# A two-layer decoder trunk on one core: VectorE alone sums all 2048 columns of the first weighted-sum stage

## The chip, the core and the metric

The program runs on one core of a Trainium2 chip. The metric is the device time of one execution in microseconds (us), lower is better; the median of several runs is taken. Engines: TensorE (PE), VectorE (DVE), ScalarE (ACT), GpSimd (POOL) and SyncE (SP). TensorE's granted clock is printed as a share of 2.4 GHz.

## The reference, cut to what matters

The trunk has 256 tokens of width 2048 (two blocks of 128 tokens) and two layers: a mixer, then a PEER expert layer, each added to the residual. All data is float32. The change touches the expert layer, in which each token picks 128 experts (8 heads by 16) and sums their value rows:

```python
def one_block(xb):                                   # xb: 128 tokens x 2048
    q = (xb @ w_q).reshape(BLOCK, PEER_HEADS, 2, PEER_HALF)
    s = jnp.einsum('thcd,hcnd->thcn', q, sub_keys)
    top_s, top_i = lax.top_k(s, PEER_TOPK)           # 16 of 128, twice per head
    ...                                              # 16 of the 256 pairs: eidx, gate g
    ue = u[eidx]                                     # 128 experts per token, rows of 2048
    ve = v[eidx]
    act = gelu(einsum('thkd,td->thk', ue, xb))
    return einsum('thk,thkd->td', g * act, ve)
```

## The kernel before, in words

Tokens lie on the 128 partitions. For one block of tokens and one layer, expert slot n (0 to 127) is one gather: GpSimd issues an indirect DMA (line 511) that brings, for each of the 128 tokens, one row of 2048 floats, 1 MB in all, into one of the 8 buffers of `ring`. A gather waits until its buffer has been used: `ring_free` (counted by VectorE) and, where TensorE reads the ring too, `pe_freed`.

The gathers form one sequence of eight phases of 128 slots, two for each of (layer 0, block 0), (layer 0, block 1), (layer 1, block 0), (layer 1, block 1). Even phases gather rows of `u`: VectorE takes a dot product with `H` for each slot (`expert_dots`, line 1391). Odd phases gather rows of `v`: the rows are summed, weighted, into the residual `X` (`expert_sum`, `weigh`, line 1400). The first weighted-sum stage is phase 1, the second and third are phases 3 and 5, and the last is phase 7.

In phases 1, 3 and 5 the sum is shared. `SHARED` gives the first shared slot. Ahead of it VectorE adds all 2048 columns of a row. From it on VectorE adds columns 0 to 1023, and TensorE adds columns 1024 to 2047 into two banks of PSUM (`weigh_part`, line 995: two matmuls for each slot, with a diagonal matrix of the slot's weights as the stationary operand). ScalarE makes these diagonals (`diagonals`, line 629), one for each slot, in 8 buffers. After slot 127 VectorE waits for TensorE and adds the two banks to `X` (line 1471), which counts `merged`; the next layer's work on ScalarE (`squares`) and TensorE (`spread_gain`) waits for `merged`.

Between the slots VectorE also does what the other block of tokens needs. `paced` hands out one piece of such work after every fourth slot at the places listed; in phase 1 these are 13 pieces of the routing of block 1 (`route`, `experts`, `gates`), after slots 35, 39, 47, 51, 59, 63, 71, 75, 83, 87, 95, 99 and 107. The last of them counts `routed`. SP, which streams the weight matrices through four buffers (`load_rows` and the loads of `w_in1` at line 430), waits for `routed` at the start of layer 1; GpSimd waits for it ahead of the gathers of phase 2; so does TensorE. On ScalarE the exponential of the gates (`gate_exp`) stands in program order behind the diagonals of slots 32 to 99, and the diagonals of slots 100 to 127 behind it.

Of the kernel before, what the change touches and what calls it, by code (L numbers as in the profile page):

```python
# [35 lines left out]
SLOTS = PEER_H * PEER_K  # L36
# [27 lines left out]

SHARED = {1: 32, 3: 24, 5: 24}
DVE_COLS = 1024
XBANKS = (1, 2, 3)
DIAGS = 8  # L70
# [43 lines left out]
def shared_before(phase, n=0):  # L114

    return sum(SLOTS - j for p, j in SHARED.items() if p < phase) + (max(n - SHARED[phase], 0) if phase in SHARED else 0)

# [6 lines left out]
def program(nc, x, positions, norm_mix0, w_in0, sinks0, conv_w0, w_out0, norm_ffn0, peer_wq0,  # L124
# [10 lines left out]
    with ctx:  # L135
# [3 lines left out]
        def sem(name):  # L139
            return ctx.enter_context(nc.semaphore(name))  # L140
# [105 lines left out]
        def bank(i, n=1, w=512):  # L246
            return ps[:, i * 512:(i + n - 1) * 512 + w]
# [9 lines left out]
        def landings(phase, n):  # L257

            return 16 * ((phase * SLOTS + n) // RING + 1)
# [37 lines left out]
        wgt_ready, diag_ready, pe_freed, merged = sem("wgt_ready"), sem("diag_ready"), sem("pe_freed"), sem("merged")  # L297
# [227 lines left out]
        def _(act):  # L525
# [30 lines left out]
            def copy_all_queries(layer, b):  # L556

                act.wait_ge(chunk_done, chunk_before(f"wq{layer}", b) + 1)
                for c in range(4):
                    nc.scalar.copy(Q1[:, c * CH:(c + 1) * CH], bank(c)).then_inc(chunk_copied, 1)  # L560
                copy_transposes(f"q{layer}", b)
# [51 lines left out]
            def gate_exp(layer, b):  # L613
                act.wait_ge(best_ready, layer * NB + b + 1)
                nc.scalar.activation(gate[:, b, :], gate[:, b, :], ACT.Exp).then_inc(gexp_done, 1)
# [6 lines left out]
            def diagonals(phase, n0, n1):  # L622

                act.wait_ge(wgt_ready, (phase + 1) // 2)
                for n in range(n0, n1):
                    k = shared_before(phase, n)
                    if k >= DIAGS:
                        act.wait_ge(pe_freed, k - DIAGS + 1)
                    nc.scalar.activation(diag[k % DIAGS], ident[:, :], ACT.Identity,  # L629
                                         scale=wgt[:, n:n + 1]).then_inc(diag_ready, 1)  # L630
# [64 lines left out]
            copy_transposes("h1", 1)  # L695
            gelus(0, 0)
            copy_all_queries(0, 1)
            diagonals(1, SHARED[1], 100)
            gate_exp(0, 1)
            diagonals(1, 100, SLOTS)  # L700

            for b in range(NB):
                act.wait_ge(merged, b + 1)
# [28 lines left out]
                copy_all_queries(1, b)  # L732
                diagonals(3 + 2 * b, SHARED[3 + 2 * b], 100)
                gate_exp(1, b)
# [21 lines left out]
        def _(pe):  # L756
# [228 lines left out]

            def weigh_part(phase):

                n0 = SHARED[phase]
                for n in range(n0, SLOTS):
                    k = shared_before(phase, n)  # L990
                    pe.wait_ge(diag_ready, k + 1)
                    pe.wait_ge(landed[n % RING], landings(phase, n))
                    for c in range(2):
                        at = DVE_COLS + c * CH
                        last = nc.tensor.matmul(bank(4 + c), diag[k % DIAGS], ring[:, n % RING, at:at + CH],  # L995
                                                start=(n == n0), stop=(n == SLOTS - 1))
                    last.then_inc(pe_freed, 1)

            def key_scores(keys, count, phase):
                for g in range(2 * PEER_H):  # L1000
                    last = nc.tensor.matmul(ps[:, g * NKEY:(g + 1) * NKEY], PQT[:, g, :], keys[:, g, :],
                                            start=True, stop=True)
                last.then_inc(rs_done, 1)
                weigh_part(phase)
                pe.wait_ge(routed, count)
# [158 lines left out]
        def _(dve):  # L1164
# [24 lines left out]
            def norm(n):  # L1189
                blocks = NORMS[n][1]  # L1190
                inverse_root(slice(blocks[0], blocks[-1] + 1), D, sq_done, norm_before(n + 1), var_ready,
                             root_ready, n + 1)
                if n in (0, 1, 3):
                    dve.wait_ge(gain_loaded, 16 * min(n + 1, 2))
                else:
                    dve.wait_ge(gain_spread, max(n - 2, 1))
                if n == 8:
                    dve.wait_ge(lifted, 12)
                spread = last_gain if n == 8 else gain[:, :] if n in (0, 1, 3) else bank(4 * ((n + 1) % 2), 4)
                for b in blocks:  # L1200
                    V.scalar_tensor_tensor(out=H[:, b, :], in0=X[:, b, :],  # L1201
                                           scalar=stat[:, 5, b:b + 1],
                                           in1=spread, op0=ALU.mult, op1=ALU.mult).then_inc(h_ready, 1)
                dve.wait_ge(h_ready, norm_before(n + 1))

            def rope(v, cos, sin, tmp):

                _, blocks, heads, dim = v.shape
                half = dim // 8
                a, b_ = v[:, :, :, 0:half], v[:, :, :, half:2 * half]  # L1210
                step = HALF_ROT // half
                shape = [P, blocks, heads, half]
                cs = cos[:, :, 0:HALF_ROT:step].unsqueeze(2).broadcast_to(shape)
                sn = sin[:, :, 0:HALF_ROT:step].unsqueeze(2).broadcast_to(shape)
                t = [tmp[:, i, 0:blocks * heads * half].rearrange("p (b h d) -> p b h d", b=blocks, h=heads)
                     for i in range(4)]
                V.tensor_tensor(t[0], a, cs, ALU.mult)
                V.tensor_tensor(t[1], b_, sn, ALU.mult)
                V.tensor_tensor(t[2], b_, cs, ALU.mult)
                link(V.tensor_tensor(t[3], a, sn, ALU.mult))  # L1220
                V.tensor_tensor(a, t[0], t[1], ALU.subtract)
                link(V.tensor_tensor(b_, t[2], t[3], ALU.add))
# [172 lines left out]
            def weigh(b, phase, i, s, weight):  # L1395
                dve.wait_ge(ring_free, i * PEER_K + (phase * SLOTS + s + RING))
                dve.wait_ge(landed[s % RING], i * 32 + 16 * (phase * SLOTS // RING + s // RING + 1))
                cols = DVE_COLS if i * PEER_K + s >= SHARED.get(phase, SLOTS) else D
                acc = last_x if phase == 7 else X[:, b, 0:cols]
                V.scalar_tensor_tensor(out=acc, in0=ring[:, s % RING, 0:cols], scalar=weight, in1=acc,  # L1400
                                       op0=ALU.mult, op1=ALU.add).then_inc(ring_free, 1)

            def last_weigh(phase):

                n = SLOTS - 1
                dve.wait_ge(ring_free, phase * SLOTS + n + RING)
                dve.wait_ge(landed[n % RING], landings(phase, n))
                for i in range(2):
                    cols = slice(i * 1024, (i + 1) * 1024)
                    last = V.scalar_tensor_tensor(out=last_x[:, cols], in0=ring[:, n % RING, cols], scalar=wgt[:, n:n + 1],  # L1410
                                                  in1=last_x[:, cols], op0=ALU.mult, op1=ALU.add)
                    last.then_inc(half_summed, 1)
                dve.wait_ge(half_summed, 2)
                dve.nop(nofuse=True).then_inc(ring_free, 1)
# [37 lines left out]
            def expert_sum(b, phase, between=None):  # L1452

                if between:
                    for n in range(SLOTS):
                        weigh(b, phase, n // PEER_K, n % PEER_K, wgt[:, n:n + 1])
                        if n % 4 == 3:
                            between(n // 4)
                else:
                    with dve.Fori(0, PEER_H - 1) as i:  # L1460
                        for s in range(PEER_K):
                            weigh(b, phase, i, s, wgt[:, bass.ds(i * PEER_K + s, 1)])
                    norm(8)
                    for n in range(SLOTS - PEER_K, SLOTS - 1):
                        weigh(b, phase, n // PEER_K, n % PEER_K, wgt[:, n:n + 1])
                    last_weigh(phase)
                dve.wait_ge(ring_free, (phase + 1) * SLOTS + RING)
                if phase in SHARED:
                    dve.wait_ge(pe_freed, shared_before(phase, SLOTS))
                    cols = X[:, b, DVE_COLS:D]  # L1470
                    V.tensor_tensor(cols, part, cols, ALU.add).then_inc(merged, 1)
                    dve.wait_ge(merged, (phase + 1) // 2)
# [208 lines left out]
```

## Time and profile before

| | |
|---|---|
| median of 3 runs | 3301.86 us (3299.7 to 3306.68) |
| the profiled execution's own time | 3302.28 us |
| its span | 3300.3 us |
| VectorE busy | 2401.2 us, 73% |
| TensorE busy | 1683.4 us, 51% |
| GpSimd busy | 1514.8 us, 46% |
| ScalarE busy | 333.7 us, 10% |
| moved by DMA | 1319.82 MB, mean 400 GB/s |

The span runs from the first to the last instruction; the execution's own time is 2 us longer. The busy shares are averages over stages that differ. Each phase is read by itself: the DMA share and the GB/s of a stretch say whether the transfers were at their rate, and the idle time in front of an engine's instructions, with what ended it, says for whom it waited.

### The profile page before, as it was taken

To read this page: it belongs to the slowest core of one execution; us is meant where nothing else is said; L and a number is where in the kernel's file an instruction comes from. 1 tells how busy PE (TensorE), PEld (TensorE's weight loads), DVE (VectorE), ACT (ScalarE), POOL (GpSimd) and SP (SyncE) were. 2 spreads that over 40 slices of the span, in tenths; PEclk is the share of its full clock that TensorE was granted. 3 is DMA by queue.
4 is the path that set the end of the run, shared out by engine and by line. 5 is a ranking of instruction groups with operands and counts; after the bars stand their busy time and mean duration, and the time that the engine had idled before them with its cause. 6 is when DMAs were issued, how large, how long until landed. Compare 5 with 4: busy or idle time off the path is not lost.

```text
span 3300.3 us, 18324 instructions
## 1 busy us (share of the span) xinstructions
PE 1683.4 (51%) x5280; PEld 844.2 (26%) x5280; DVE 2401.2 (73%) x2771; ACT 333.7 (10%) x783; POOL 1514.8 (46%) x1042
## 2 busy tenths in 40 slices
PE   7995466575577662547377763556277700000000
PEld 4955322232222231323122232332122200000000
DVE  1129674676777568866977577966976689999999
ACT  1110000110111101100111112110011100000000
POOL 0105342353565545644766544644756643333332
PEclk9997799788899996779699977788699955555555
DMA  9669799899999999999999999999999999999997
GB/s 336 229 242 411 295 421 420 349 394 421 422 421 421 419 420 411 411 416 421 422 421 420 421 419 414 388 422 422 421 422 421 422 422 422 421 422 421 422 422 332
DMA packets 215948, 1319.82 MB, mean 400 GB/s; under 512 B 23536, under 2 KB 23600, under 8 KB 70832
## 3 DMA queue, kind: packets, MB, share of 16 engines
q0 software_dynamic: 147728, 1074.86, 78.7%
q1 hardware_dynamic: 68128, 243.86, 18.7%
q8 instruction: 43, 0.70, 0.1%
q14 instruction: 49, 0.40, 0.0%
HBM read 1316.54 MB, written 2.10 MB: 400 GB/s over the span
## 4 chain that ended last, share of the span: by engine, by line
issue 29%; POOL 21%; DMA 20%; PE 16%; DVE 12%; ACT 2%; DVEq 0%; POOLq 0%; PEldq 0%; SPq 0%; ACTq 0%
POOL ring L511 21%; DMA ring<-in_peer_v,eidx 10%; DVE ps L1400 9%; PE ps L995 7%; DMA A<-in_w_in 4%; PE ps L795 3%; PE ps L811 3%; DMA ring<-in_peer_u,eidx 3%; DMA A<-in_peer_wq 2%; PE ps L945 1%; PE ps L791 1%; ACT A L629 1%; DVE X L1400 1%; ACT KT L629 1%; PE ps L1016 0%
## 5 line engine op out<-in xcount | busy, mean ns | idle before, releaser
L511 POOL DMA_INDIRECT ring<-in_peer_u,eidx x512 | 762.8, 1490 | 965.2 <-DVE dots L1391 797.0
L1391 DVE CUSTOM_DVE_ANT_0 kdup<-ring,H 128x2048 bf16<-128x2048 f32 x384 | 880.0, 2292 | 286.8 <-DMA ring<-in_peer_u,eidx 279.4
L511 POOL DMA_INDIRECT ring<-in_peer_v,eidx x512 | 734.2, 1434 | 641.0 <-DVE ps L1400 189.9
L1400 DVE SCALAR_TENSOR_TENSOR X<-ring,wgt,X 128x1024 f32<-128x1024 f32 (+1 forms) x384 | 578.6, 1507 | 263.6 <-DMA ring<-in_peer_v,eidx 253.7
L995 PE MATMUL ps<-ring,KT 128*128 128x512 f32 x608 | 302.0, 622 | 209.9 <-DMA ring<-in_peer_v,eidx 147.3
L995 PE MATMUL ps<-ring,A 128*128 128x512 f32 x608 | 297.1, 611 | 92.2 <-ACT A L629 48.7
L1400 DVE SCALAR_TENSOR_TENSOR ps<-ring,wgt,ps 128x2048 f32<-128x2048 f32 x127 | 299.1, 2355 | 18.4 <-DVE ps L1400 5.2
L1391 DVE CUSTOM_DVE_ANT_0 kdup<-ring,ps 128x2048 bf16<-128x2048 f32 x128 | 292.8, 2288 | 21.2 <-DMA ring<-in_peer_u,eidx 15.6
L995 PEld LDWEIGHTS ps<-ring,KT 128*128 128x128 f32 x608 | 106.4, 194 | 403.6 <-issue 244.7
L774 PE MATMUL ps<-ident,gainT 128*128 128x128 f32 x192 | 25.5, 298 | 322.5 <-DVE wgt L1447 319.2
L995 PEld LDWEIGHTS ps<-ring,A 128*128 128x128 f32 x608 | 103.1, 189 | 286.2 <-ACT A L629 125.1
L774 PEld LDWEIGHTS ps<-ident,gainT 128*128 128x128 f32 x192 | 24.6, 211 | 326.4 <-issue 326.4
L629 ACT ACTIVATE KT<-ident,wgt 128x128 f32<-128x128 f32 x152 | 60.1, 403 | 433.6 <-PE ps L995 433.6
L945 PE MATMUL ps<-PR,HT 128*128 128x512 f32 x144 | 69.3, 621 | 65.9 <-issue 37.5
L851 PE MATMUL ps<-PR,HT 128*128 128x512 f32 x192 | 87.7, 602 | 21.1 <-DMA PR<-in_peer_wq 19.8
L811 PE MATMUL ps<-HT,ring 128*128 128x128 f32 x768 | 88.7, 278 | 1.6 <-ACT PR L642 1.0
L629 ACT ACTIVATE A<-ident,wgt 128x128 f32<-128x128 f32 x152 | 59.7, 401 | 291.7 <-PE ps L995 291.7
L811 PEld LDWEIGHTS ps<-HT,ring 128*128 128x128 f32 x768 | 87.4, 194 | 3.4 <-ACT PR L642 1.9
L901 PE MATMUL ps<-ident,A 128*128 128x128 f32 x96 | 19.4, 359 | 121.0 <-ACT A L595 120.1
L759 PE MATMUL ps<-ident,H 128*128 128x128 f32 x140 | 28.4, 387 | 97.1 <-DVE H L1201 96.0
L488 POOL TENSOR_TENSOR PR<-PR 128x1024 f32<-128x1024 f32 x1 | 2.3, 2347 | 129.6 <-ACT PR L651 129.6
L1520 DVE TENSOR_TENSOR X<-ps,X 128x512 f32<-128x512 f32 x4 | 2.8, 691 | 76.8 <-PEq L781 76.8
(291 smaller groups left out, 1990.7 us busy)
## 6 DMA issues: line engine op xcount, KB each, us to landing
ring<-in_w_in SPq DMA_DIRECT2D x18, 2048.0 KB, 12.3
PR<-in_peer_wq SPq DMA_DIRECT2D x32, 1024.0 KB, 16.1
PR<-in_w_out SPq DMA_DIRECT2D x24, 1024.0 KB, 13.7
PR<-in_w_in SPq DMA_DIRECT2D x24, 768.0 KB, 14.6
ring<-in_w_out SPq DMA_DIRECT2D x8, 2048.0 KB, 9.4
A<-in_peer_wq SPq DMA_DIRECT2D x16, 1024.0 KB, 16.1
A<-in_w_out SPq DMA_DIRECT2D x12, 1024.0 KB, 12.4
A<-in_w_in SPq DMA_DIRECT2D x12, 768.0 KB, 14.6
```

The source lines that it names most:

```text
L511: pool.indirect_dma_start(ring[:, n % RING, :], None, table, bass.IndirectOffsetOnAxis(eidx[:, b, n:n + 1], 0)).then_inc(landed[n % RING], 16)
L629: nc.scalar.activation(diag[k % DIAGS], ident[:, :], ACT.Identity, scale=wgt[:, n:n + 1]).then_inc(diag_ready, 1)
L759: last = nc.tensor.transpose(ps[:, bank0 * 512 + i * P:bank0 * 512 + (i + 1) * P], s, ident[:, :])
L774: last = nc.tensor.matmul(ps[:, at:at + P], gainT[:, i, k:k + 1].broadcast_to([P, P]), ident[:, :], start=True, stop=True)
L791: last = nc.tensor.matmul(bank(4 * (m % 2) + g, w=tokens), tile[:, k, g * P:(g + 1) * P], lhs[:, kk, :], **flags)
L795: last = nc.tensor.matmul(bank(4 * (m % 2) + b, w=width), lhs[:, kk, b * P:(b + 1) * P], tile[:, k, 0:width], **flags)
L811: last = nc.tensor.matmul(ps[:, at:at + P], wtile(slot)[:, k, c:c + P], HT1[:, 8 * t + k, :], start=(t == k == 0), stop=(t == 1 and k == 7))
L851: last = nc.tensor.matmul(bank(bank0 + c), lhs[:, k, :], rows[n % WSLOTS][:, c * CH:(c + 1) * CH], start=(k == 0), stop=(k == KT_ - 1))
L945: last = nc.tensor.matmul(bank(bank0 + c), HT1[:, k, :], rows_l0[n % WSLOTS][:, c * CH:(c + 1) * CH], start=(k == 0), stop=(k == KT_ - 1))
L995: last = nc.tensor.matmul(bank(4 + c), diag[k % DIAGS], ring[:, n % RING, at:at + CH], start=(n == n0), stop=(n == SLOTS - 1))
L1391: V.tensor_tensor_reduce(out=junk, in0=ring[:, s % RING, :], in1=last_h if phase == 6 else H[:, b, :], scale=1.0, scalar=0.0, op0=ALU.mult ...
L1400: V.scalar_tensor_tensor(out=acc, in0=ring[:, s % RING, 0:cols], scalar=weight, in1=acc, op0=ALU.mult, op1=ALU.add).then_inc(ring_free, 1)
```

## The change

`SHARED` loses its entry for phase 1, so in that phase every slot counts as unshared: VectorE adds all 2048 columns of all 128 rows. TensorE's loop over the slots of phase 1 is empty, ScalarE's two calls of `diagonals` for phase 1 are gone, and instead of the addition that merged TensorE's half, an empty VectorE instruction counts `merged` after the last slot. Phases 3 and 5 stay as they are (their diagonals are counted from 0 in place of 96, a multiple of 8, so the same buffers serve the same slots).

```diff
-SHARED = {1: 32, 3: 24, 5: 24}
+SHARED = {3: 24, 5: 24}
@@ ScalarE
             copy_all_queries(0, 1)
-            diagonals(1, SHARED[1], 100)
             gate_exp(0, 1)
-            diagonals(1, 100, SLOTS)
@@ TensorE, weigh_part
-                n0 = SHARED[phase]
+                n0 = SHARED.get(phase, SLOTS)
                 for n in range(n0, SLOTS):
@@ VectorE, expert_sum
                 dve.wait_ge(ring_free, (phase + 1) * SLOTS + RING)
+                if phase == 1:
+                    dve.nop(nofuse=True).then_inc(merged, 1)
                 if phase in SHARED:
                     dve.wait_ge(pe_freed, shared_before(phase, SLOTS))
```

Line numbers of the changed kernel are lower by 2 or 3 behind the ScalarE edit. On VectorE, at the start of phase 1, the rows of the kernel before are these (`X<-ring,wgt,X` is the weighted addition of a slot, the others are pieces of the routing):

```order
L1400 SCALAR_TENSOR_TENSOR X<-ring,wgt,X 128x2048 x32
L1400 SCALAR_TENSOR_TENSOR X<-ring,wgt,X 128x1024 x4
L1278 MAX A<-ps 128x8 x16
L1400 SCALAR_TENSOR_TENSOR X<-ring,wgt,X 128x1024 x4
L1282 MAX_INDEX A<-A,ps 128x8 x16
```

and of the changed kernel these:

```order
L1398 SCALAR_TENSOR_TENSOR X<-ring,wgt,X 128x2048 x36
L1276 MAX A<-ps 128x8 x16
L1398 SCALAR_TENSOR_TENSOR X<-ring,wgt,X 128x2048 x4
L1280 MAX_INDEX A<-A,ps 128x8 x16
L1398 SCALAR_TENSOR_TENSOR X<-ring,wgt,X 128x2048 x8
```

The pieces stand behind the same slots; the additions from slot 32 on have 2048 columns in place of 1024. On the same engine at the end of phase 1, before:

```order
L1350 TENSOR_TENSOR gate<-gate,gsum 128x128
L1400 SCALAR_TENSOR_TENSOR X<-ring,wgt,X 128x1024 x20
L1471 TENSOR_TENSOR X<-ps,X 128x1024
L1391 ISA kdup,dots<-ring,H 128x2048
L1391 ISA dots 128x1
```

and in the changed kernel:

```order
L1348 TENSOR_TENSOR gate<-gate,gsum 128x128
L1398 SCALAR_TENSOR_TENSOR X<-ring,wgt,X 128x2048 x20
L1389 ISA kdup,dots<-ring,H 128x2048
L1389 ISA dots 128x1
```

The merging addition is gone (the empty instruction in its place stands in no row), and the first dot product of phase 2 (`kdup,dots<-ring,H`) follows the last slot. On TensorE the changed kernel goes from the routing's scores (L999) straight to the work that waits for `merged` (L772):

```order
L862 MATMUL ps<-ident,HT 128x128 x16
L999 MATMUL ps<-PR 128x128 x16
L772 MATMUL ps<-ident,gainT 128x128 x16
L757 MATMUL ps<-ident,H 128x128 x16
L1092 MATMUL ps<-PR,HT 128x512
```

Before, 192 matmuls of 512 columns (L995), two for each of 96 slots, stood between the second and the third of these rows; the trace counts each float32 matmul twice, so that it shows 384 of them. Nothing else moved on TensorE.

## Rows read from the trace of the kernel before

**Rows 1.** Windows: stretch, length; PE, PEld, DVE, ACT, POOL; clock, DMA, GB/s.

```profile
891.60:1141.10 249.50, 188.71 (x384) 65.87 (x384) 174.26 (x302) 36.48 (x90) 143.33 (x97) 0.99 1.01 421
1142.00:1180.00 38.00, 24.48 (x88) 15.31 (x88) 36.27 (x37) 5.83 (x8) 27.87 (x15) 0.82 1.01 420
1142.00:1530.00 388.00, 199.61 (x636) 110.08 (x637) 295.67 (x324) 48.21 (x118) 197.77 (x118) 0.77 1.01 415
2650.00:2968.00 318.00, 0.43 (x2) 0.46 (x3) 295.61 (x266) 3.47 (x6) 119.88 (x129) 0.50 1.01 422
1300.00:1340.00 40.00, 5.55 (x30) 5.36 (x30) 39.13 (x51) 1.50 (x8) 28.31 (x15) 0.59 0.97 380
```

**Rows 2.** Page, section 2: 40 slices of the span, busy tenths and GB/s.

```profile
DMA  9669799899999999999999999999999999999997
GB/s 336 229 242 411 295 421 420 349 394 421 422 421 421 419 420 411 411 416 421 422 421 420 421 419 414 388 422 422 421 422 421 422 422 422 421 422 421 422 422 332
```

**Rows 3.** Waits of VectorE, 785 to 1142 us: total, times, longest.

```profile
DVE X L1400 <- DMA ring<-in_peer_v,eidx: 95.5, 69, 2.6
...
DVE X L1471 <- PE ps L995: 0.8, 1, 0.8
```

**Rows 4.** Waits of VectorE, 1142 to 1530 us.

```profile
DVE kdup L1391 <- DMA ring<-in_peer_u,eidx: 81.8, 45, 2.7
...
DVE stat L1181 <- ACT A L711: 1.8, 1, 1.8
```

**Rows 5.** Timeline of VectorE, phase 1: start, duration, instruction, idle before.

```profile
791.62 23.84 DVE L1400 SCALAR_TENSOR_TENSOR X<-ring,wgt,X 128x2048 f32<-128x2048 f32 x10
...
894.09 1.28 DVE L1400 SCALAR_TENSOR_TENSOR X<-ring,wgt,X 128x1024 f32<-128x1024 f32 x1 [1.20 <-DMA ring<-in_peer_v,eidx]
...
900.25 3.26 DVE L1278 MAX8 A<-ps 128x8 f32<-128x128 f32 x16
```

**Rows 6.** Timeline of VectorE, end of phase 1.

```profile
1092.62 1.29 DVE L1400 SCALAR_TENSOR_TENSOR X<-ring,wgt,X 128x1024 f32<-128x1024 f32 x1 [2.39 <-DMA ring<-in_peer_v,eidx]
1096.18 1.29 DVE L1400 SCALAR_TENSOR_TENSOR X<-ring,wgt,X 128x1024 f32<-128x1024 f32 x1 [2.27 <-DMA ring<-in_peer_v,eidx]
...
1136.53 1.28 DVE L1400 SCALAR_TENSOR_TENSOR X<-ring,wgt,X 128x1024 f32<-128x1024 f32 x1 [1.21 <-DMA ring<-in_peer_v,eidx]
1139.01 1.28 DVE L1400 SCALAR_TENSOR_TENSOR X<-ring,wgt,X 128x1024 f32<-128x1024 f32 x1 [1.20 <-DMA ring<-in_peer_v,eidx]
1141.12 1.23 DVE L1471 TENSOR_TENSOR X<-ps,X 128x1024 f32<-128x1024 f32 x1 [0.82 <-PE ps L995]
1142.38 2.29 DVE L1391 CUSTOM_DVE_ANT_0 kdup<-ring,H 128x2048 bf16<-128x2048 f32 x1
```

**Rows 7.** Timeline of TensorE, phase 1.

```profile
891.65 6.91 PE L995 MATMUL ps<-ring,KT 128*128 128x512 f32 x12 [22.26 <-DMA ring<-in_peer_v,eidx]
...
937.35 1.95 PE L995 MATMUL ps<-ring,KT 128*128 128x512 f32 x4 [0.53 <-ACT KT L629]
```

**Rows 8.** Line 1400 alone, same columns as rows 1 for VectorE.

```profile
891.60:1141.10 249.50, 123.34 (x96) 0.99 1.01 421
```

**Rows 9.** Groups of VectorE, 785 to 1142 us: count | busy, mean | idle.

```profile
L1400 DVE SCALAR_TENSOR_TENSOR X<-ring,wgt,X 128x1024 f32<-128x1024 f32 x96 | 123.3, 1285 | 74.3 <-DMA ring<-in_peer_v,eidx 72.9
L1400 DVE SCALAR_TENSOR_TENSOR X<-ring,wgt,X 128x2048 f32<-128x2048 f32 x32 | 75.3, 2352 | 24.6 <-DMA ring<-in_peer_v,eidx 22.5
```

**Rows 10.** Issues of SP, 1060 to 1142 us, then the DMA view.

```profile
1082.92 0.89 SPq L430 DMA_DIRECT2D PR<-in_w_in  x2
...
PR<-in_w_in SPq DMA_DIRECT2D x2, 848.0 KB, 14.5
A<-in_w_in SPq DMA_DIRECT2D x1, 848.0 KB, 25.0
MT<-in_w_in SPq DMA_DIRECT2D x1, 848.0 KB, 31.2
```

**Rows 11.** Timeline of GpSimd, phase 1: gather issues.

```profile
794.24 2.93 POOL L511 DMA_INDIRECT ring<-in_peer_v,eidx  x1 [11.39 <-DVE X L1400]
797.48 2.08 POOL L511 DMA_INDIRECT ring<-in_peer_v,eidx  x1 [0.30 <-issue]
799.87 2.08 POOL L511 DMA_INDIRECT ring<-in_peer_v,eidx  x1 [0.30 <-issue]
...
1076.36 1.01 POOL L511 DMA_INDIRECT ring<-in_peer_v,eidx  x1 [0.30 <-issue]
1077.68 1.01 POOL L511 DMA_INDIRECT ring<-in_peer_v,eidx  x1 [0.30 <-issue]
...
1091.72 0.94 POOL L511 DMA_INDIRECT ring<-in_peer_v,eidx  x1 [2.20 <-PE ps L995]
```

**Rows 12.** Timeline of GpSimd, phase 7.

```profile
3258.38 0.94 POOL L511 DMA_INDIRECT ring<-in_peer_v,eidx  x1 [1.46 <-DVE ps L1400]
```

**Rows 13.** Line 511, issue to landing: 1300 to 1340 us, then the whole span.

```profile
DMA to landing us min/median/max: 9.2/9.9/14.3
...
DMA to landing us min/median/max: 6.5/17.0/38.0
```

**Rows 14.** TensorE, `spread_gain` after phase 1 and after long idling.

```profile
1142.49 3.81 PE L774 MATMUL ps<-ident,gainT 128*128 128x128 f32 x32 [1.48 <-DVE X L1471]
...
2967.57 6.56 PE L774 MATMUL ps<-ident,gainT 128*128 128x128 f32 x32 [319.19 <-DVE wgt L1447]
```

## The prediction

> **What bounds the kernel now.** I read the windows first. From 891.6 to 1141.1 us, which are slots 32 to 127 of phase 1, the DMA share is 1.01 at 421 GB/s, while VectorE is busy 174.26 of 249.5 us. It is much the same in the phases behind (415 GB/s from 1142 to 1530 us, 422 from 2650 to 2968 us) [rows 1], and in most of the 40 slices [rows 2]. So the kernel is bound by its transfers: from phase 1 on the DMA engines have next to no idle time in which they could catch up, and a microsecond in which they starve is a microsecond of the end. The waits say the same from the other side: in phase 1 VectorE idles 95.5 us for gathers to land, and 0.8 us for TensorE at the merge [rows 3]. VectorE starts a slot every 2.49 us (1136.53, 1139.01) and works 1.28 us of it [rows 6]; TensorE takes 1.95 us for its half [rows 7]. Both are faster than the gather.
>
> The question is therefore one only: can VectorE by itself keep up with a gather every 2.49 us, with its pieces of routing among the slots?
>
> **The change part by part.**
>
> *VectorE's additions.* A full-width slot, back to back, costs 23.84 / 10 = 2.384 us [rows 5], against 2.352 us for the instruction alone [rows 9]. That is 0.1 us under the gather's 2.49. So slots without a piece among them only just keep up. The 96 slots from 32 on take 96 x 2.384 = 228.9 us, where they take 123.34 us now [rows 8].
>
> *The pieces.* In the same window VectorE is busy 174.26 us in all [rows 1], 123.34 of them line 1400 [rows 8]; the other 174.26 - 123.34 = 50.9 us are the routing. They now lie in the 1.2 us holes ahead of each slot [rows 5, 6] and cost nothing. With full-width additions the holes are gone, and they stand on the path.
>
> *Sum on VectorE.* 228.9 + 50.9 = 279.8 us from 891.65 us, where TensorE takes up slot 32 [rows 7], so the last slot is done at 1171.4 us. Today the last slot is done at 1139.01 + 1.28 = 1140.3, and the first dot product of phase 2 starts at 1142.38, behind TensorE's last half (0.82 us of idle) and the merge (1.23 us) [rows 6]. These 2.1 us go away, and nothing is late in their place: the row that is needed next has landed by then, or is the gather priced below. So phase 2 starts 1171.4 - 1142.4 = 29 us later by VectorE's own time.
>
> *What the ring can take up.* Eight buffers let the transfers run ahead of VectorE, but no more than that. They run ahead from slot 35 on, and after some ten slots with pieces all buffers hold landed rows and the DMA engines go idle. This buys nothing at the end of the phase, since there the transfers are the slower side again: after slot 107 come 20 slots without a piece (47.7 us on VectorE), and beside their gathers SP brings the four tiles of `w_in1`, 4 x 848 KB [rows 10], which at 421 GB/s are 8.3 us. 20 x 2.49 + 8.3 = 58 us of transfers in 48 us of VectorE: the ring is drained by slot 127, as today.
>
> *How late a freed buffer is filled.* After starving, the transfers need one gather's latency to start again. Where VectorE is the slow side today, a gather lands 9.9 us after its issue at the median, against 17.0 us when the queue is full and 6.5 us at the least [rows 13]. I ran the recursion for both (a gather lands at the later of freed + latency and last landing + 2.49; VectorE starts at the later of landed and free). Its first form, which counts each piece's overlap with its neighbour twice (13 x 0.11 = 1.4 us), gives a DMA idle time of 31.4 us with a latency of 6.6 and 34.8 with 10; less 1.4 us it is 30.0 and 33.4 us. Its bound from below is VectorE's 29 us. I take 31 us, nearer to VectorE's own sum, which comes from rows without a model.
>
> *GpSimd.* Its issue of a gather takes 2.08 us while VectorE runs full-width additions from `ring` and `X`, 1.0 us between short instructions [rows 11], and 0.94 us where VectorE's accumulator is in PSUM [rows 12]. So one gather is issued for each full-width addition (2.08 + 0.30 = 2.38 us), as many as buffers come free: it adds latency, which the last step holds, and no rate. The Trainium skill ("SBUF — State Buffer", Who interferes with whom) says that a VectorE instruction with two SBUF inputs contends only with GpSimd instructions that read SBUF, and infers that descriptor generation, which writes, is not held. The rows above disagree: the issue is held. By the page the latency would be the short one, 6.5 us, and the sum 30; by the row it is 31 to 33.
>
> *ScalarE and TensorE.* The 96 diagonals and 192 matmuls cost nothing now, hidden under the transfers (DMA share 1.01 [rows 1]), and give nothing when they go. The exponential of the gates no longer waits behind diagonals; the routing piece that needs it comes after slot 107, long after, so 0. TensorE will have idled for some 300 us when phase 2 begins. After idling as long, `spread_gain` takes 6.56 us, with the granted clock at 0.50 (1.2 GHz) up to there, in place of 3.81 [rows 1, 14]. The norm that needs them comes after four dot products (over 9 us), so this is hidden. The first matmuls of `w_in1` behind it may be late by 2 to 4 us; VectorE's wait in the low-rank norm, 1.8 us now [rows 4], can grow by that, but VectorE idles 81.8 us for gathers in that phase [rows 4] and the ring covers a stall of a few us. I take 0 and keep 4 us for the upper end.
>
> *Is it given back later?* VectorE's time is: it has the 81.8 us. The transfers' time isn't: in the phases behind they run at 415 to 422 GB/s with or without the change [rows 1].
>
> *Total.* 3302.28 + 31 = 3333.3 us for the profiled execution; the median lies 0.4 us lower, so 3333 us. Own range: 29 us less 3 of error in the sum at the bottom, 33.4 + 4 and 1 at the top: 3328 to 3340.
>
> **The rivals.**
>
> *A. The ring and the later idle time take it all up, no change.* For it: 95.5 us of idle VectorE in the phase. The idle time here is 74.3 us at the shared slots [rows 9], the work added 96 x (2.384 - 1.285) = 105.5 us, so 105.5 - 74.3 = 31 us do not fit, which is the same sum by another way. For it to be hidden the transfers would have to have slack behind, against rows 1. Then the time is 3302.3 less the 2.1 us of the merge: 3300. Chance 0.05.
>
> *B. GpSimd becomes the bound.* An issue held by VectorE needs 2.08 + 0.30 = 2.38 us, just VectorE's pitch. If it kept missing its turn and every issue took 2.93 us, as the first one of such a run does [rows 11], plus 0.30, then 96 slots take 96 x 3.23 = 310 us in place of 249.5, less the merge: +58, 3360. Against it: ten slots at full width keep 2.38 without a miss [rows 5, 11], and short instructions let it catch up at 1.3 us each [rows 11]. It decides from the point where issues fall behind the freed buffers by more than the ring. Chance 0.04.
>
> *C. Faster.* TensorE holds the ring. Around 1091.72 us GpSimd waits 2.20 us for TensorE, not for VectorE [rows 11], and slots come every 3.6 us there (1092.62, 1096.18 [rows 6]), eight of them. If that were TensorE's doing, taking it out would give 8 x (3.6 - 2.49) = 8.9 us and the 2.1 of the merge, if VectorE kept up: 3291. It decides if VectorE's lag stays under the ring's eight slots. Against it: the tiles of `w_in1` are issued at 1082.92 us [rows 10] and their 8.3 us are the same 8.9 us; TensorE waits for the gather too. Chance 0.03.
>
> *D. A cold TensorE delays phase 2.* It would show in phase 2 as longer waits of VectorE for ScalarE and TensorE; from 1300 to 1340 us the transfers already drop to 380 GB/s with VectorE busy 39.13 of 40 us [rows 1], so a late mixer there would starve them. TensorE is busy 24.48 us from 1142 to 1180 us at a mean clock of 0.82 [rows 1]; at 0.50 throughout that is 24.48 x 0.82 / 0.50 = 40 us, 16 us more. If 10 of them weren't covered: 3343. Chance 0.08.
>
> **How the numbers follow.** The forecast has 0.80, A 0.05, B 0.04, C 0.03, D 0.08. The range reaches from 3323 to 3344: the forecast's own range, D, and 5 us below for a routing that overlaps more than its busy time shows. A measurement of this kernel tells 0.2% (6.6 us) from no change. Slower by more: forecast, B, D, 0.92 in all. Within it: A, 0.05. Faster: C, 0.03.
>
> **What would show it.** In the profile after, line 1400 has 128 instructions of 2048 columns in phase 1 with a mean of 2.35 us and, from slot 36 on to about 115, no wait for a gather; the wait for `in_peer_v` in phase 1 falls from 95.5 to some 25 us. GpSimd waits for VectorE ahead of most issues. The transfers fall below 421 GB/s between some 970 and 1130 us, with 31 us of starving in all (about 375 GB/s over the stretch from 891 to 1171 us), and are at 421 again by 1140. The first dot product of phase 2 starts near 1172 us, and each phase behind it ends 29 to 33 us later than before, with its own length kept. The prediction is wrong if VectorE still waits for gathers between the pieces; if phase 2 or a later one becomes shorter, so that some is given back; or if the stretch from slot 32 to slot 127 takes over 290 us, which would point to GpSimd.

## The result and the profile after

The changed kernel takes 3336.73 us (median of 4 runs, 3332.82 to 3344.16), the kernel before 3302.8 us beside it. The ratio is 1.0104, with a 95% interval of 1.0091 to 1.0117. That is 34 us slower, where 31 were forecast. The profiled execution took 3334.28 us, 32.0 us more than that of before, with a span of 3332.5 us.

The windows of the changed kernel (columns as in [rows 1]) cut the stretch of slots 32 to 127 into pieces of about 40 us, and the last row is phase 2 at the same length as in [rows 1]:

```profile
891.60:930.00 38.40, 0.00 (x0) 0.00 (x0) 37.61 (x61) 0.00 (x0) 26.54 (x14) 0.50 1.01 422
930.00:970.00 40.00, 0.00 (x0) 0.00 (x0) 39.50 (x63) 0.00 (x0) 27.77 (x15) 0.50 0.93 375
970.00:1010.00 40.00, 0.00 (x0) 0.00 (x0) 39.50 (x55) 0.00 (x0) 27.27 (x14) 0.50 0.83 325
1010.00:1050.00 40.00, 0.00 (x0) 0.00 (x0) 39.57 (x54) 0.00 (x0) 27.37 (x14) 0.50 0.95 371
1050.00:1090.00 40.00, 0.00 (x0) 0.00 (x0) 39.47 (x35) 0.31 (x1) 25.95 (x12) 0.50 0.90 364
1090.00:1130.00 40.00, 0.00 (x0) 0.00 (x0) 39.33 (x22) 0.00 (x0) 29.21 (x13) 0.50 0.74 299
1130.00:1173.00 43.00, 0.00 (x0) 0.00 (x0) 41.68 (x18) 0.01 (x1) 37.51 (x19) 0.50 1.02 421
...
1173.00:1561.00 388.00, 204.25 (x630) 113.32 (x630) 294.15 (x323) 48.21 (x118) 200.60 (x119) 0.75 1.01 418
```

The third busy figure is VectorE's: 37.6 us of 38.4, then 39.5 of 40, with no room left. The last figure is the transfers' rate. It holds at 422 GB/s for the first 38 us, in which the ring absorbs the lag, falls for 200 us, and is back at 421 in the last 43 us, where no pieces lie. Where the rate was 421 throughout in [rows 1], the missing part comes to 40 x (5 - (375 + 325 + 371 + 364 + 299) / 421) = 35 us.

Phase 2 starts only 30.9 us later, so some 4 us of the missing transfers are not paid for there. From the weights of phase 1 to the first dot product of phase 2 the changed kernel moves 145.58 MB and the kernel before 147.70 MB, and almost all of the 2.1 MB between them are gathers (5.0 us at 421 GB/s). Phase 2 moves 1.0 MB more than before in the same 388 us (162.20 against 161.20 MB, the 418 GB/s against 415). Almost all of that (0.9 MB) is moved in one place: from 1307 to 1346 us the kernel before transfers at 379 GB/s, with VectorE busy 38.21 of 39 us, and the changed kernel has 402 GB/s from 1338 to 1377 us, the same place 31 us later. There the transfers had time to spare, and 2 to 3 us of the lag go into it.

The waits of VectorE from 785 to 1173 us answer to [rows 3]:

```profile
DVE X L1398 <- DMA ring<-in_peer_v,eidx: 23.0, 10, 2.6
DVE wgt L1447 <- ACT score L619: 5.9, 1, 5.9
```

Of 95.5 us of waiting for gathers 23.0 are left, ten waits, and these lie ahead of slot 32. The timeline of VectorE at the end of the phase answers to [rows 6]:

```profile
1116.65 7.13 DVE L1398 SCALAR_TENSOR_TENSOR X<-ring,wgt,X 128x2048 f32<-128x2048 f32 x3
1123.69 0.28 DVE L1346 TENSOR_REDUCE gsum<-gate 128x8 f32<-128x128 f32 x1
1124.01 0.20 DVE L1347 RECIPROCAL gsum<-gsum 128x8 f32<-128x8 f32 x1
1124.25 0.29 DVE L1348 TENSOR_TENSOR gate<-gate,gsum 128x128 f32<-128x128 f32 x1
1124.57 48.32 DVE L1398 SCALAR_TENSOR_TENSOR X<-ring,wgt,X 128x2048 f32<-128x2048 f32 x20
1173.14 2.29 DVE L1389 CUSTOM_DVE_ANT_0 kdup<-ring,H 128x2048 bf16<-128x2048 f32 x1 [0.25 <-DMA ring<-in_peer_u,eidx]
```

The first dot product of phase 2 starts at 1173.14 us in place of 1142.38. Of GpSimd this is what the issues look like around a piece of routing (937.4 to 941.7 us; the first addition behind it ends at 944.1), and below it, from the view of line 511, how long a gather took to land, from 900 to 1100 us:

```profile
936.18 2.09 POOL L511 DMA_INDIRECT ring<-in_peer_v,eidx  x1 [0.30 <-issue]
938.58 0.93 POOL L511 DMA_INDIRECT ring<-in_peer_v,eidx  x1 [0.30 <-issue]
944.37 2.93 POOL L511 DMA_INDIRECT ring<-in_peer_v,eidx  x1 [4.86 <-DVE X L1398]
```

```profile
DMA to landing us min/median/max: 6.6/8.0/16.3
```

Behind the piece GpSimd waits 4.86 us for VectorE to free a buffer. A gather lands 8.0 us after its issue at the median, near the least of the kernel before (6.5 us) and far from its median of 17.0 [rows 13].

### The profile page after: what moved, and what is told of

Same layout as the page of the kernel before. It is cut to its first block, busy times and chain, and to the rows that moved or that the text cites. A ratio compares the mean times of both kernels' runs of the same rounds, so it can differ in the third digit from the quotient of the medians.

```text
span 3332.5 us, 17114 instructions
## 1 busy us (share of the span) xinstructions
PE 1505.3 (45%) x4896; PEld 784.4 (24%) x4896; DVE 2502.4 (75%) x2770; ACT 296.3 (9%) x687; POOL 1583.4 (48%) x1042
## 4 chain that ended last, share of the span: by engine, by line
DMA 25%; issue 22%; DVE 19%; POOL 17%; PE 15%; ACT 2%; DVEq 0%; POOLq 0%; PEldq 0%; SPq 0%; ACTq 0%
POOL ring L511 17%; DMA ring<-in_peer_u,eidx 10%; DVE ps L1398 9%; DMA ring<-in_peer_v,eidx 8%; DVE X L1398 5%; PE ps L993 5%; DMA HT<-in_w_in 5%; PE ps L793 3%; PE ps L809 3%; DMA HT<-in_peer_wq 2%; DVE kdup L1389 1%; PE ps L943 1%; PE ps L789 1%; PE ps L978 0%; ACT KT L629 0%
## 5 line engine op out<-in xcount | busy, mean ns | idle before, releaser
L511 POOL DMA_INDIRECT ring<-in_peer_u,eidx x512 | 773.1, 1510 | 952.2 <-DVE dots L1389 785.3
L1389 DVE CUSTOM_DVE_ANT_0 kdup<-ring,H 128x2048 bf16<-128x2048 f32 x384 | 880.0, 2292 | 287.2 <-DMA ring<-in_peer_u,eidx 279.8
L511 POOL DMA_INDIRECT ring<-in_peer_v,eidx x512 | 792.4, 1548 | 619.3 <-DVE ps L1398 191.0
L1398 DVE SCALAR_TENSOR_TENSOR X<-ring,wgt,X 128x1024 f32<-128x1024 f32 (+1 forms) x384 | 681.0, 1774 | 193.8 <-DMA ring<-in_peer_v,eidx 181.0
L772 PE MATMUL ps<-ident,gainT 128*128 128x128 f32 x192 | 26.6, 305 | 624.0 <-DVE wgt L1445 319.4
L993 PE MATMUL ps<-ring,KT 128*128 128x512 f32 x416 | 205.9, 620 | 159.0 <-DMA ring<-in_peer_v,eidx 115.5
L993 PE MATMUL ps<-ring,A 128*128 128x512 f32 x416 | 203.3, 611 | 61.2 <-ACT A L629 35.7
L772 PEld LDWEIGHTS ps<-ident,gainT 128*128 128x128 f32 x192 | 25.7, 218 | 627.4 <-issue 627.4
L993 PEld LDWEIGHTS ps<-ring,KT 128*128 128x128 f32 x416 | 72.1, 192 | 291.6 <-issue 176.0
L993 PEld LDWEIGHTS ps<-ring,A 128*128 128x128 f32 x416 | 70.4, 189 | 194.0 <-ACT A L629 93.2
L849 PE MATMUL ps<-PR,HT 128*128 128x512 f32 x192 | 93.9, 638 | 20.7 <-DMA PR<-in_peer_wq 19.4
L943 PE MATMUL ps<-PR,HT 128*128 128x512 f32 x144 | 69.8, 623 | 64.5 <-issue 37.6
L629 ACT ACTIVATE KT<-ident,wgt 128x128 f32<-128x128 f32 x104 | 41.1, 401 | 312.8 <-PE ps L993 312.8
L978 PE MATMUL ps<-PR,MT 128*128 128x512 f32 x128 | 59.2, 617 | 2.7 <-ACT MT L611 2.7
```

The lines of the kernel that those rows point to most:

```text
L511: pool.indirect_dma_start(ring[:, n % RING, :], None, table, bass.IndirectOffsetOnAxis(eidx[:, b, n:n + 1], 0)).then_inc(landed[n % RING], 16)
L772: last = nc.tensor.matmul(ps[:, at:at + P], gainT[:, i, k:k + 1].broadcast_to([P, P]), ident[:, :], start=True, stop=True)
L849: last = nc.tensor.matmul(bank(bank0 + c), lhs[:, k, :], rows[n % WSLOTS][:, c * CH:(c + 1) * CH], start=(k == 0), stop=(k == KT_ - 1))
L943: last = nc.tensor.matmul(bank(bank0 + c), HT1[:, k, :], rows_l0[n % WSLOTS][:, c * CH:(c + 1) * CH], start=(k == 0), stop=(k == KT_ - 1))
L978: last = nc.tensor.matmul(bank(4 + c), MT1[:, k, :], rows_l1[n % WSLOTS][:, c * CH:(c + 1) * CH], start=(k == 0), stop=(k == KT_ - 1))
L1389: V.tensor_tensor_reduce(out=junk, in0=ring[:, s % RING, :], in1=last_h if phase == 6 else H[:, b, :], scale=1.0, scalar=0.0, op0=ALU.mult ...
```

## The experiments

Each ratio is to the kernel before, timed on the same chip. The profiled executions differ by up to 9 us in what they take before phase 1, which no edit here touches. So the traces are compared by the length of phase 1, from the moment VectorE computes the weights of phase 1 (`wgt<-score,gate`) to the first dot product of phase 2. That is 1142.38 - 791.29 = 351.1 us before and 1173.14 - 791.15 = 382.0 us in the changed kernel, 30.9 more. Each such length comes from one execution. Those of the runs that leave phase 1 at its old speed lie between 349.9 and 351.8 us, so a difference under 2 us says nothing.

### Both engines' work, and VectorE at full width

```diff
 # the kernel before, VectorE's additions
-cols = DVE_COLS if i * PEER_K + s >= SHARED.get(phase, SLOTS) else D
+cols = DVE_COLS if phase > 1 and i * PEER_K + s >= SHARED.get(phase, SLOTS) else D
 # the merge of phase 1: an empty instruction that counts merged
```

> The kernel before, but in phase 1 VectorE adds all 2048 columns from slot 32 on, while TensorE and ScalarE still do their 96 diagonals and 192 matmuls (the sums are dropped: an empty instruction in place of the merge). Theory: what costs is VectorE's width alone. Phase 2 starts at 1173 to 1176 us in place of 1142.4, and the time is that of the changed kernel, ratio to before 1.009 to 1.012 (3333 to 3342 us). Rival (a TensorE that idled and is cold, or work whose cover is gone, makes up part of the loss): with TensorE busy as before, the ratio is under 1.006 (under 3323 us).

Measured: 3335.66 us, ratio 1.0098 (1.0079 to 1.0118), phase 1 of 1174.86 - 791.51 = 383.4 us. Its window answers to the first of [rows 1]:

```profile
891.60:1141.10 249.50, 174.84 (x340) 62.58 (x340) 245.92 (x290) 34.46 (x86) 170.53 (x84) 0.94 0.90 361
```

TensorE is at work (174.84 us) with a clock of 0.94 and ScalarE makes its diagonals, and still the transfers fall to 361 GB/s. The whole loss is there with nothing taken from the other engines. VectorE's width makes it. Phase 1 is 1.4 us longer than in the changed kernel, and the phases behind it are 3.0 us shorter (2997.61 - 1174.86 = 1822.8 us from the first dot product of phase 2 to the weights of phase 7, against 1825.8). In phase 1 the difference is two short waits for gathers behind slot 32, 1.5 us in all; why they are there, and why the phases behind are shorter, no run says. The medians (3335.66 and 3336.73 us) can't be told apart.

### TensorE's part left out, VectorE at half width

```diff
 # the changed kernel, VectorE's additions
-cols = DVE_COLS if i * PEER_K + s >= SHARED.get(phase, SLOTS) else D
+cols = DVE_COLS if i * PEER_K + s >= (32 if phase == 1 else SHARED.get(phase, SLOTS)) else D
```

> The changed kernel, but VectorE adds only columns 0 to 1023 from slot 32 of phase 1 on, as before, and nobody adds the other 1024 (this half of the first sum is left out for 96 slots). TensorE and ScalarE idle in phase 1. Theory: TensorE's and ScalarE's part was hidden under the transfers, so without it the time is that of before less at most the 2.1 us of the merge: ratio 0.998 to 1.001, DMA at 421 GB/s through the phase. Rival cold TensorE: phase 2 becomes longer, ratio 1.002 or more. Rival (TensorE held the ring around 1090 us): 3291 us, ratio 0.997 or less.

Measured: 3302.61 us, ratio 0.9994 (0.9984 to 1.0003), phase 1 of 349.9 us. In the trace of this kernel VectorE's wait in phase 1 and the windows are:

```profile
DVE X L1398 <- DMA ring<-in_peer_v,eidx: 95.4, 69, 2.6
```

```profile
891.60:1141.10 249.50, 0.00 (x0) 0.00 (x0) 175.73 (x303) 0.31 (x1) 112.81 (x98) 0.50 1.01 421
```

```profile
1142.00:1180.00 38.00, 26.73 (x88) 17.69 (x87) 35.43 (x35) 5.42 (x8) 27.81 (x14) 0.75 1.02 421
```

The same wait as before the change (95.4 against 95.5 us), the same rate of transfers: TensorE's and ScalarE's part cost nothing in phase 1. TensorE enters phase 2 from a clock of 0.50, runs at 0.75 in its first 38 us where it ran at 0.82, and is busy 26.73 us for 24.48 [rows 1]. These 2 us don't show in the time: from the first dot product of phase 2 to the weights of phase 7 pass 2968.96 - 1142.74 = 1826.2 us, against 1825.4 before, and this length lies between 1822.8 and 1826.6 us in all the traces here. This puts an end to the rival of a cold TensorE at the size that it was given (10 us), and, since taking TensorE off the ring gains nothing, to the one that it held the gathers.

### VectorE with 1536 columns, TensorE with 512

```diff
 # the kernel before; in phase 1 from slot 32 on
-cols = DVE_COLS if ... else D
+cols = (1536 if phase == 1 else DVE_COLS) if shared else D
-for c in range(2):                              # TensorE
+for c in range(1 if phase == 1 else 0, 2):
 # the merge of phase 1 adds columns 1536 to 2047 only
```

> The kernel before, but in phase 1 VectorE adds 1536 columns from slot 32 on and TensorE 512 (one matmul a slot). Theory: VectorE's sum is 96 x about 1.85 + 50.9 = 228 us, under the 249 us of the transfers, so the ring covers nearly all: phase 2 starts 0 to 3 us later, ratio 1.000 to 1.001. Rival (each added column costs, in proportion, as where GpSimd's issue is held for the length of each addition): half of the loss, 15 to 17 us, ratio 1.005.

Measured: 3301.9 us, ratio 0.9995 (0.9986 to 1.0005), phase 1 of 351.8 us. The group of the 96 additions, columns as in [rows 9], and the window:

```profile
L1401 DVE SCALAR_TENSOR_TENSOR X<-ring,wgt,X 128x1536 f32<-128x1536 f32 x96 | 174.5, 1818 | 24.1 <-DMA ring<-in_peer_v,eidx 21.6
```

```profile
891.60:1141.10 249.50, 174.96 (x190) 43.01 (x190) 225.38 (x302) 36.50 (x90) 162.57 (x97) 0.61 1.00 415
```

Half of the added work was added, 174.5 - 123.3 = 51 us, and phase 1 is 0.7 us longer, no more than the traces scatter. VectorE's sum of 174.5 + 50.9 = 225 us lies under the 249.5 of the transfers. The price is a threshold, not a proportion. The rate of 415 GB/s instead of 421 is 249.5 x 6 / 421 = 3.6 us of missing transfers, so here too some 3 us of them are not paid for. TensorE's granted clock was 0.61 here, and its matmuls took longer, 174.96 us for half as many; this cost nothing either.

### Full width from slot 108 on

```diff
 SHARED = {1: 32, 3: 24, 5: 24}
+END = {1: 108, 3: 128, 5: 128}      # used by both engines, the diagonals and the counts
```

> The kernel before, but the sharing of phase 1 ends at slot 107, the last slot with a piece of routing behind it: slots 108 to 127 are full width on VectorE. Theory: a full-width slot costs 2.384 us against 2.49 us a gather, so where no piece lies among the slots and the tiles of w_in1 slow the gathers further, full width is free: phase 2 starts 0 to 1.5 us later, ratio 0.999 to 1.001. Rival (full width costs wherever it stands): 20/96 of the loss, 6.5 us, ratio 1.002.

Measured: 3302.63 us, ratio 0.9998 (0.9988 to 1.0007), phase 1 of 350.4 us. VectorE's timeline in this kernel:

```profile
1083.08 4.81 DVE L1402 SCALAR_TENSOR_TENSOR X<-ring,wgt,X 128x2048 f32<-128x2048 f32 x2 [0.48 <-DMA ring<-in_peer_v,eidx]
1088.69 2.35 DVE L1402 SCALAR_TENSOR_TENSOR X<-ring,wgt,X 128x2048 f32<-128x2048 f32 x1 [0.81 <-DMA ring<-in_peer_v,eidx]
...
1110.34 2.35 DVE L1402 SCALAR_TENSOR_TENSOR X<-ring,wgt,X 128x2048 f32<-128x2048 f32 x1 [1.20 <-DMA ring<-in_peer_v,eidx]
1114.07 27.00 DVE L1402 SCALAR_TENSOR_TENSOR X<-ring,wgt,X 128x2048 f32<-128x2048 f32 x11 [1.38 <-DMA ring<-in_peer_v,eidx]
```

VectorE still waits for gathers between full-width additions. The long waits lie where the tiles of `w_in1` slow the gathers to one in 3.6 us; the last 11 additions start 2.46 us apart on average ((27.00 - 2.35) / 10), nearer to the gathers' 2.49 than to VectorE's 2.384. So in the last 20 slots, where no piece of routing lies, full width is free.

### Sharing from slot 64 on

```diff
-SHARED = {1: 32, 3: 24, 5: 24}
+SHARED = {1: 64, 3: 24, 5: 24}
```

> The kernel before, but phase 1 is shared from slot 64 on in place of 32: 32 more slots are full width, six pieces of routing lie behind them (after slots 35 to 63). Theory, by the recursion of the prediction (a gather lands at the later of freed buffer + 9 to 10 us and last landing + 2.49 us): VectorE needs 32 x 2.4 + 23.8 = 100.6 us where the gathers need 80.5, so 20 us too many; the ring holds back some 10 of them; phase 2 starts 9 to 10 us later and the ratio is 1.003. Rival (the whole excess counts, the ring gives nothing): 20 us, ratio 1.006. Rival (proportional to slots): 32/96 of 31 us, 10 us, which this run can't tell from the first; the run with a full-width tail does that.

Measured: 3310.72 us, ratio 1.0031 (1.0020 to 1.0042), phase 1 of 1149.01 - 789.97 = 359.0 us, 8.0 more than before; 9 to 10 were expected. The windows show where:

```profile
930.00:970.00 40.00, 0.00 (x0) 0.00 (x0) 39.50 (x63) 0.00 (x0) 28.09 (x14) 0.50 0.94 375
970.00:1010.00 40.00, 25.14 (x49) 9.23 (x50) 39.43 (x79) 4.82 (x12) 24.86 (x18) 0.89 0.92 359
1010.00:1141.00 131.00, 95.63 (x197) 33.20 (x196) 86.64 (x100) 18.82 (x46) 71.22 (x51) 1.00 1.01 421
```

By the sum above VectorE has 20 us too much, and the kernel loses 8: in this one trace the ring takes up 12 us, once. VectorE idles 44 of the 131 us behind (86.64 busy) and the loss stays. Idle time of VectorE afterwards gives nothing back, since the transfers are at their rate (421 GB/s) there.

### The sum in PSUM

```diff
 # the changed kernel; ScalarE copies X to four banks before phase 1, and back after it
-acc = last_x if phase == 7 else X[:, b, 0:cols]
+acc = last_x[:, 0:cols] if phase in (1, 7) else X[:, b, 0:cols]
```

> The changed kernel, but the sum of phase 1 is kept in four banks of PSUM (ScalarE copies X there beforehand and back afterwards), as phase 7 does, so that the additions have one input in SBUF, and GpSimd's issue should take 0.94 us instead of 2.08. Theory: VectorE's pitch is the same (2.39 us), so the loss is the same but for some of the latency: phase 2 starts at 1170 to 1174 us, ratio to before 1.008 to 1.010. Rival (GpSimd's held issues make a good part of the loss): phase 2 starts before 1165 us, ratio 1.006 or less.

Measured: 3332.88 us, ratio 1.0091 (1.0076 to 1.0107), phase 1 of 1173.67 - 792.01 = 381.7 us, 0.3 less than in the changed kernel. The timeline of GpSimd at the same place as above:

```profile
936.24 0.94 POOL L512 DMA_INDIRECT ring<-in_peer_v,eidx  x1 [1.45 <-DVE ps L1405]
938.63 0.94 POOL L512 DMA_INDIRECT ring<-in_peer_v,eidx  x1 [1.45 <-DVE ps L1405]
945.26 0.94 POOL L512 DMA_INDIRECT ring<-in_peer_v,eidx  x1 [5.69 <-DVE ps L1405]
```

GpSimd's issue is 0.94 us again in place of 2.08 and 2.93, and the ratio can't be told from that of the changed kernel (their intervals overlap). The held issue is real, and it is not what the kernel waits for. The time from issue to landing is the same as well, 7.9 us against 8.0 (median, 900 to 1100 us), so this run doesn't say what a shorter latency would be worth.

### The pieces packed

```diff
-ROUTE_AT = (8, 9, 11, 12, 14, 15, 17, 18, 20, 21, 23, 24, 26)
+ROUTE_AT = (8, 9, 10, 11, 12, 13, 14, 15, 16, 17, 18, 19, 20)
```

> The changed kernel, but the 13 pieces of routing come after every fourth slot from 35 to 83, not spread out to 107. The count of instructions is the same. Theory, by the recursion: while the pieces last the transfers starve, and behind slot 83 VectorE is the faster side again and idles, so a little is lost more: phase 2 starts at 1175 to 1178 us, ratio 1.010 to 1.011. Rival 1 (only VectorE's sum counts, wherever the pieces lie): 1173 us, 1.0095. Rival 2 (the 8.3 us of w_in1 tiles, issued earlier since the last piece is earlier, fill time in which the gathers starve): the ratio falls to 1.0075 (3327 us).

Measured: 3342.51 us, ratio 1.0115 (1.0099 to 1.0130), phase 1 of 1184.59 - 798.96 = 385.6 us, 3.6 more than the changed kernel. This execution reached phase 1 7.8 us later than that of the changed kernel. Its windows from shortly ahead of the last piece (which ends at 1076 us) are:

```profile
1050.00:1090.00 40.00, 0.00 (x0) 0.00 (x0) 39.37 (x21) 0.00 (x0) 27.55 (x13) 0.50 0.72 287
1090.00:1130.00 40.00, 0.00 (x0) 0.00 (x0) 38.18 (x18) 0.00 (x0) 35.12 (x17) 0.50 1.02 422
1130.00:1173.00 43.00, 0.00 (x0) 0.00 (x0) 40.72 (x18) 0.00 (x0) 37.55 (x18) 0.50 1.01 422
```

The same instructions take longer: in the last 83 us VectorE idles 4 us, where it idled 2 in the last 83 of the changed kernel. Of the 3.6 us, 1.0 lies ahead of slot 32, where the two kernels are the same; some 2.7 us remain. So this trace says that it isn't VectorE's sum alone that counts: where VectorE gets ahead of the gathers again, it idles, and its work isn't done sooner. The medians don't show it by themselves (1.0099 to 1.0130 against 1.0091 to 1.0117), and it stays the reading of one trace. The tiles of `w_in1` were issued at 1076 us, when the starving ended, and filled none of it.

### The mixer's pieces spread out

```diff
-MIX_AT = (0, 4, 7, 8, 11, 12, 13, 15, 17, 19, 21, 24, 25)
+MIX_AT = (0, 4, 7, 9, 11, 13, 15, 17, 19, 21, 22, 24, 25)
```

> The kernel before, with another list of places for the mixer's pieces in phases 2 and 4: the pieces after places 8, 12, 13, 15, 17, 19, 21 come one or two places (4 to 8 slots) later, so that fewer lie close together. In the trace of before the transfers drop to 380 GB/s from 1300 to 1340 us and lower still around 2060 us, where these pieces lie close. Theory (a cluster of pieces starves the transfers once the ring is used up, and lost transfer time is never given back): some of the 3 + 8 us come back, 3297 to 3301 us, ratio 0.9985 to 0.9995. Rival (spreading moves the starving elsewhere or makes the output projection late): 1.000 to 1.003.

Measured: 3303.65 us, ratio 1.0003 (0.9994 to 1.0012), no difference; the expected gain of 2 to 6 us did not come. From 1290 to 1350 us and from 2010 to 2130 us its trace shows what stands below the dots; above them is the kernel before, from 2010 to 2130 us:

```profile
2010.00:2130.00 120.00, 49.43 (x191) 35.39 (x192) 111.07 (x145) 22.47 (x54) 81.62 (x42) 0.67 0.97 393
...
1290.00:1350.00 60.00, 14.83 (x101) 13.00 (x99) 58.69 (x74) 10.95 (x32) 45.56 (x24) 0.64 0.99 397
2010.00:2130.00 120.00, 27.07 (x122) 21.65 (x122) 111.42 (x143) 15.73 (x37) 81.22 (x42) 0.61 0.97 391
```

The transfers starve about as much as before (397 and 391 GB/s, where the kernel before has 394 and 393 in the same stretches; this trace is 5.8 us later at the start of phase 2). So the new places did not thin out the starving, and the run doesn't test whether less of it would be paid back. My attempt to use the lesson on the kernel before gained nothing; which other places would, I haven't tried. No version here beats the kernel before.

## Why the prediction was right

**What bounds.** As forecast, nearly all that the transfers starve is lost for good. Phases 2 to 6, from the first dot product of phase 2 to the weights of phase 7, last 2967.80 - 1142.38 = 1825.4 us before and 2998.91 - 1173.14 = 1825.8 us after. These are the rows of the weights, before and after:

```profile
2967.80 0.29 DVE L1449 TENSOR_TENSOR wgt<-score,gate 128x128 f32<-128x128 f32 x1 [0.38 <-ACT score L619]
...
2998.91 0.29 DVE L1447 TENSOR_TENSOR wgt<-score,gate 128x128 f32<-128x128 f32 x1 [0.38 <-ACT score L619]
```

The rule that a microsecond of starving is a microsecond of the end is a little too strict. The prediction's list of signs has 31 us of starving at about 375 GB/s; it was 35 us at 368 GB/s (891.6 to 1171 us), and 31 to 32 us were paid. The prediction had that nothing is given back; phase 2 took some 3 us of transfers into a stretch with time to spare, while every phase kept its length.

**VectorE's sum.** Forecast 228.9 + 50.9 = 279.8 us from slot 32 on, with slot 127 done at 1171.4 us. Measured, from 891.6 to 1173.0 us VectorE is busy 276.67 us of 281.4, and slot 127 ends at 1124.57 + 48.32 = 1172.9. The first 76 slots with the pieces took 1124.57 - 891.72 = 232.9 us, 0.8 more than 76 x 2.384 + 50.9 = 232.1. The last 20 took 48.32 us in place of 47.7, since the ring is drained behind slot 120: the last additions start (14.77 - 2.35) / 5 = 2.48 us apart, at the gathers' pace, as this row of the end of the phase shows.

```profile
1158.12 14.77 DVE L1398 SCALAR_TENSOR_TENSOR X<-ring,wgt,X 128x2048 f32<-128x2048 f32 x6
```

**Latency of a freed buffer.** The recursion was run with 6.6 and 10 us and gave 30.0 and 33.4; the measured latency is 8.0 us from the issue, and phase 1 is 30.9 us longer. The figure of 31 was right, and in part by luck: it was chosen between VectorE's own 29 us and the recursion, to pay for gathers that land late. Of the 2 us between 29 and 31, late gathers took 0.9 (0.6 in the last 20 slots and 0.25 ahead of the first dot product), and 0.8 is VectorE's work that the sum had too small. What a shorter latency would be worth, no run shows.

**The merge.** The 2.1 us of it went: the dot product follows the last slot by 0.25 us.

**The given nothings.** TensorE's and ScalarE's work was hidden (left out: 0.9994; kept: 1.0098), and the cold clock cost nothing that can be seen. In the first 37 us of phase 2 TensorE is busy 24.02 us at a mean clock of 0.86 in the changed kernel, no longer than the 24.48 us at 0.82 before [rows 1]:

```profile
1173.00:1210.00 37.00, 24.02 (x88) 16.12 (x88) 33.92 (x34) 5.82 (x8) 28.67 (x15) 0.86 1.01 420
```

VectorE's wait for gathers in phase 2 is 84.8 us, against 81.8 before [rows 4].

**The rivals.** A (the ring takes it all up) falls by the result, though the ring takes up some 12 us of VectorE's lag, once, as the run shared from slot 64 shows. B (GpSimd) falls by the stretch from slot 32 to slot 127, 281 us and not over 290, and by the run with PSUM. C and D fall by the run with TensorE's part left out. The rule of the Trainium skill ("SBUF — State Buffer", Who interferes with whom), by which descriptor generation is inferred to go on beside an addition with two SBUF inputs, disagrees with the traces: 2.08 us with both inputs in SBUF, 0.94 with the accumulator in PSUM, at the same slots. Its other statement, that such an addition contends with a GpSimd instruction that reads SBUF, fits both if a gather's issue reads its row numbers (`eidx`, a tile in SBUF) there. No run here tells whether it is that read or the writing of descriptors that is held.

**What is off.** One sign came otherwise. GpSimd was to wait for VectorE ahead of most issues; it does so ahead of 12 of 97 (53.5 us), and the others start 0.3 us behind the one before, because the issue itself is held for the length of an addition. With the sum in PSUM, where it isn't held, 97 of 98 issues wait for VectorE. The transfers began to fall at 940 us (422 GB/s from 930 to 940 us, 348 from 940 to 950), not at some 970. The medians differ by 34 us, the traces by 32; the interval of the ratio (1.0091 to 1.0117, 30 to 39 us) holds both, so the 2 us can't be told from scatter.

## What to carry to other kernels

Where the transfers bound, compare each engine's cost per arriving tile, with the side work that shares it, to the transfer's own time for a tile: here 2.384 us against 2.49, and 50.9 us of side work that turned a margin into 31 us. An engine's idle time hides extra work only where the two lie close together. What exceeds it by more than the buffers can hold (about 12 us here, once) is lost, unless a stretch behind has transfer time to spare (3 us here). The engine's idle time afterwards gives nothing back while the transfers are at their rate. Below that threshold extra work is free: 51 us more on VectorE cost nothing, and the last 20 slots, which have no side work, needed no help from TensorE.

## What the runs showed of the hardware

A gather's issue on GpSimd takes 2.08 us while VectorE adds with both inputs in SBUF back to back (2.93 us for the first of a run) and 0.94 us when the accumulator is in PSUM. The rate of the transfers was the same either way while VectorE was the slow side (361 and 363 GB/s from 900 to 1100 us). With one matmul of 512 columns a slot in place of two, TensorE's granted clock over the stretch was 0.61 instead of 0.99, and it was busy nearly as long for half of the work (174.96 us for 188.71).
